# Attention of a hybrid decoder block on pairs of heads, with one step for mask, scale and row extreme, and the merge's rounding on ScalarE

## What is computed

```
merged = sigmoid(gate_a) * (out_a @ w_proj_a) + sigmoid(gate_b) * (out_b @ w_proj_b)
x = x + gate1 * (merged @ w_out)
h2 = rms_norm(x) * (1 + scale2) + shift2
x = x + gate2 * (square(relu(h2 @ w_mlp1 + b_mlp1)) @ w_mlp2 + b_mlp2)
```

## Time and profile before

| | us |
|---|---|
| median of three runs (963.65 to 968.84) | 968.44 |
| the profiled execution, its own time | 967.11 |
| its span, first to last instruction | 965.4 |
| TensorE busy | 878.1 (91%) |
| VectorE busy | 464.7 (48%) |
| ScalarE busy | 335.9 (35%) |
| mean granted TensorE clock, share of full | 0.950 |

### The profile page before, as it was taken

One profiled execution on the slowest core, in us unless ns is written; L12 is line 12 of the kernel. 1 busy time (PEld: TensorE's weight loads), 2 busy tenths in 40 slices (PEclk: granted clock), 3 DMA queues, 4 the chain that ended last, 5 costly groups with the idle time before them and its releaser, 6 DMA issues.

```text
span 965.4 us, 10903 instructions
## 1 busy us (share of the span) xinstructions
PE 878.1 (91%) x3855; PEld 688.1 (71%) x3855; DVE 464.7 (48%) x763; ACT 335.9 (35%) x495; POOL 233.0 (24%) x125
## 2 busy tenths in 40 slices
PE   3799899899877977988899996999999999999998
PEld 2577578687766764655568874688888888888886
DVE  4914789791887784444429764643211122221000
ACT  2634452453123313665512223434312124442211
POOL 3024233334000000000000000264444444444440
PEclk9699999999989977989889998999999999999999
DMA  9912323423111112222226653263233233333302
GB/s 358 254 54 72 82 66 87 107 54 101 25 38 27 44 27 82 66 83 71 66 66 202 199 187 108 68 195 108 89 93 103 87 97 99 89 107 97 99 22 87
DMA packets 144551, 95.69 MB, mean 99 GB/s; under 512 B 8199, under 2 KB 138629, under 8 KB 143493
## 3 DMA queue, kind: packets, MB, share of 16 engines
q1 hardware_dynamic: 143104, 95.18, 33.2%
q10 hardware_dynamic: 1412, 0.07, 0.1%
HBM read 93.13 MB, written 2.10 MB: 99 GB/s over the span
## 4 chain that ended last, share of the span: by engine, by line
PE 75%; DVE 18%; DMA 2%; ACT 2%; issue 2%; SPq 0%; DVEq 0%; ACTq 0%
PE bank L1100 19%; PE bank L1101 19%; PE bank L1102 19%; PE bank L1241 3%; PE bank L1242 3%; PE bank L1243 2%; DMA ada_raw<-in_w_ada 2%; PE bank L1318 2%; PE bank L1344 2%; DVE w_lo L753 2%; DVE hg_at L909 2%; DVE hg_rt L877 1%; DVE rt_k L805 1%; PE bank L1128 1%; DVE ada_acc L972 1%
## 5 line engine op out<-in xcount | busy, mean ns | idle before, releaser
L407 POOL TENSOR_TENSOR w_lo<-w_raw,w_hi 128x1024 fp32r<-128x1024 f32 x90 | 224.1, 2489 | 703.7 <-ACT w_hi L461 703.7
L1100 PE MATMUL bank<-h_hi,w_hi 128*128 128x512 f32 x544 | 219.3, 403 | 14.0 <-DVE h_lo L783 13.5
L1101 PE MATMUL bank<-h_lo,w_hi 128*128 128x512 f32 x544 | 213.6, 393 | 0.0
L1102 PE MATMUL bank<-h_hi,w_lo 128*128 128x512 f32 x544 | 213.3, 392 | 0.0
L461 ACT ACTIVATE w_hi<-w_raw 128x1024 fp32r<-128x1024 f32 x126 | 132.7, 1053 | 166.1 <-PE bank L1102 163.5
L1100 PEld LDWEIGHTS bank<-h_hi,w_hi 128*128 128x128 f32 x544 | 102.9, 189 | 45.7 <-issue 16.9
L1101 PEld LDWEIGHTS bank<-h_lo,w_hi 128*128 128x128 f32 x544 | 103.3, 190 | 21.9 <-issue 1.7
L1102 PEld LDWEIGHTS bank<-h_hi,w_lo 128*128 128x128 f32 x544 | 103.2, 190 | 21.7
L1100 PE MATMUL bank<-u_hi,w_hi 128*128 128x512 f32 x256 | 100.0, 391 | 0.0
L1102 PE MATMUL bank<-u_hi,w_lo 128*128 128x512 f32 x256 | 99.7, 389 | 0.0
L1101 PE MATMUL bank<-u_lo,w_hi 128*128 128x512 f32 x256 | 99.6, 389 | 0.0
(11 more groups left out here) (212 smaller groups left out, 1087.1 us busy)
## 6 DMA issues: line engine op xcount, KB each, us to landing
w_raw<-in_w_mlp SPq DMA_DIRECT2D x128, 256.0 KB, 3.0
w_raw<-in_w_in SPq DMA_DIRECT2D x88, 256.0 KB, 3.3
ada_even<-in_w_ada SPq DMA_DIRECT2D x20, 512.0 KB, 4.7
ada_raw<-in_w_ada SPq DMA_DIRECT2D x8, 1024.0 KB, 9.1
ada_odd<-in_w_ada SPq DMA_DIRECT2D x8, 512.0 KB, 4.5
w_raw<-in_w_out SPq DMA_DIRECT2D x16, 256.0 KB, 3.0
x_nat<-in_x SPq DMA_DIRECT2D x4, 512.0 KB, 6.3
w_raw<-in_w_proj_a SPq DMA_DIRECT2D x8, 256.0 KB, 2.8
```

Of the source, the lines that this page charges most:

```text
L407: nc.gpsimd.tensor_tensor(w_lo[:, s], w_raw[:, s], w_hi[:, s].bitcast(F32), ALU.subtract).then_inc(lo_ready, 1)
L1100: mm(bank[b][:], w_hi[:, slot, j], rhs_hi(i), start=f, stop=False)
L1101: mm(bank[b][:], w_hi[:, slot, j], rhs_lo(i), start=False, stop=False)
L1102: end = mm(bank[b][:], w_lo[:, slot, j], rhs_hi(i), start=False, stop=l)
```

## The change

- Attention goes by pairs of heads. Logits of heads 2p and 2p+1 alternate, widest query block first (512, 512, 384, 384, ... columns), into four banks instead of two; the fifth waits for VectorE to have taken the first.
- VectorE's one step now adds the mask, scales by -1/8 and takes the row minimum, so the step that scaled the maximum (L996) is gone, and ScalarE's exponential waits for its own block alone. Reciprocals are one per block (eight of 128 x 1 for a pair) in place of one of 128 x 4 per head.
- Transposes of a pair alternate between banks 2 and 3, a block of the gate projection between them; values of the two heads alternate within the unit of a pair, on the two column halves of the array. `prT` is doubled.
- TensorE does gate block 8 before the logits of pair 0, block 9 after them, block 8+2p between the transposes of pair p-1, block 9+2p after the logits of pair p, and the b halves of projections 0 and 1 and parts of their a halves between the transposes of the last pair and around its values.
- The eight groups of two in the first projections become one each; GpSimd is not touched. Two slices of `w_ada` are asked for at the start, then 3, 3 and 2 `ada_add` stand before the mask steps of pairs 1, 2 and 3, three after the last pair, and one in each of merges 1 to 5; the buffers move, so that the second is free from the start.
- The merge: the rounding to `h_hi` is taken by ScalarE, and `split_lo` and `ada_add` stand between the sum and `h_lo`.

The core of the diff (new helper functions in full where the text speaks of them):

```diff
+        ADA_PAIR = [0, 0, 3, 6, 8, 11]
+        LOGIT_BANK = [[6, 7, 2, 3], [6, 7, 4, 5]]
+        def heads(p):
+            return [(2 * s + e, TB - 1 - s, e) for s in range(TB) for e in range(2)]
 # SyncE
             load_ada(0)
-            for m in range(KC):
-                if m + 1 < KC:
-                    load_ada(m + 1)
-                load_proj(m)
+            load_ada(1)
+            for p in range(1, PAIRS + 1):
+                load_proj(2 * p - 2)
+                load_proj(2 * p - 1)
+                for i in range(ADA_PAIR[p] + 2, ADA_PAIR[p + 1] + 2):
+                    load_ada(i)          # waits for ada_add(i - 2)
 # ScalarE
+            for p in range(PAIRS + 1):
+                if p:
+                    turned(p - 1)        # eight copies bank -> prT
+                if p < PAIRS:
+                    gate(KC + 2 * p, sig_b[:, 2 * p])
+                    for t, qb, e in heads(p):
+                        act.wait_ge(logit_masked, 8 * p + t + 1)
+                        w = pr[:, e, OFF_Q[qb]:OFF_Q[qb] + (qb + 1) * P]
+                        nc.scalar.activation(w, w, ACT.Exp, scale=-1.0, bias=..., accum_out=...)
+                    gate(KC + 2 * p + 1, sig_b[:, 2 * p + 1])
+                if p:
+                    oa_head(p - 1)
+            for m in range(KC):
+                act.wait_ge(group_done, G[U_P + m + 1])
+                split_hi(U_P + m + WS)
+                act.wait_ge(sum_ready, m + 1)
+                nc.scalar.activation(h_hi[:, m], sig_a[:, m], ACT.Copy).then_inc(mh_ready, 1)
 # VectorE
+            for p in range(PAIRS + 1):
+                if p:
+                    split_lo(U_M + KC + WS + 2 * p - 2)
+                    split_lo(U_M + KC + WS + 2 * p - 1)
+                if p >= 2:
+                    oa_low(p - 2)
+                if p < PAIRS:
+                    for i in range(ADA_PAIR[p], ADA_PAIR[p + 1]):
+                        ada_add(i)
+                    if p:
+                        dve.wait_ge(prob_turned, 8 * p)
+                    for t, qb, e in heads(p):
+                        v.tensor_tensor_reduce(out=pr[...], in0=bank[...], in1=score[:, qb, 0:n],
+                            scale=-(HD ** -0.5), scalar=-TAKEN, op0=ALU.add, op1=ALU.min, accum_out=...)
+                    for t, qb, e in heads(p):
+                        dve.wait_ge(exp_done, 8 * p + t + 1)
+                        step(v.reciprocal(s, s))
+                        v.tensor_scalar(w, w, s, None, ALU.mult).then_inc(prob_ready, 1)
+            mod_add(0)
+            ada_add(KC)
+            oa_low(PAIRS - 1)
+            ada_add(KC + 1)
+            ada_add(KC + 2)
             for m in range(KC):
                 dve.wait_ge(group_done, G[U_P + m + 1])
                 v.tensor_tensor(sa, bank[b][:], sa, ALU.mult)
                 step(v.tensor_tensor(sb, bank[b + 1][:], sb, ALU.mult))
-                step(v.tensor_tensor(sa, sa, sb, ALU.add))
-                step(v.tensor_copy(mh, sa))
+                v.tensor_tensor(sa, sa, sb, ALU.add).then_inc(sum_ready, 1)
+                if m < KC - 1:
+                    split_lo(U_P + WS + m)
+                if 1 <= m <= 5:
+                    ada_add(10 + m)
+                dve.wait_ge(mh_ready, m + 1)
                 v.tensor_tensor(ml, sa, mh.bitcast(F32), ALU.subtract).then_inc(merged_ready, 1)
-                split_lo(U_P + WS + m)
-                ada_add(KC + m)
 # TensorE
+            gate_blocks(KC, 0, 8)
+            pe.wait_ge(ort_ready, BH)
+            logits(0)
+            gate_blocks(KC + 1, 0, 8)
+            for p in range(1, PAIRS):
+                j = KC + 2 * p
+                def filler(t):           # called before the first and after each of the eight t
+                    if t == 0:
+                        gate_blocks(j, 0, 2)
+                    elif 2 <= t <= 7:
+                        gate_blocks(j, t, t + 1)
+                turn_probs(p - 1, filler)
+                logits(p)
+                gate_blocks(j + 1, 0, 8)
+                values(p - 1)
+            ... last pair: turn_probs with proj_blocks(0, 4, 8), (1, 4, 6), (1, 6, 8), (0, 0, 2)
+            mod_columns(0)
+            values(PAIRS - 1)
+            proj_blocks(0, 2, 3)
+            proj_blocks(1, 0, 3, True)
+            pe.wait_ge(oa_ready, PAIRS)
+            proj_blocks(0, 3, 4, False, True).then_inc(group_done, 1)
+            proj_blocks(1, 3, 4, False, True).then_inc(group_done, 1)
+            for m in range(2, KC):
+                pe.wait_ge(merged_ready, m - 1)
+                pe.wait_ge(lo_ready, U_P + m + 1)
+                proj_blocks(m, 4, 8, True, True)
+                proj_blocks(m, 0, 4, True, True).then_inc(group_done, 1)
```

More of the change, by code:

```diff
@@ L627, in _ @@
             gate(2 * BH - 1, sig_a[:, 2 * BH - 1])
[L630 to L653, removed]
-                        act.wait_ge(ob_ready, BH)
-                    gate(KC + h, sig_b[:, h])
@@ L658, in _, with turned @@
[L658 to L663, removed]
+            def turned(p):
+                if p:
+                    act.wait_ge(pv_done, p)
+                for t, kb, e in heads(p):
+                    act.wait_ge(prob_turned, 8 * p + t + 1)
+                    w = T - kb * P
+                    nc.scalar.activation(prT[:, e, OFF_K[kb]:OFF_K[kb] + w], bank[2 + t % 2][:, kb * P:T],
+                                         ACT.Copy).then_inc(probT_ready, 1)
@@ L1005, in _ @@
[L1005 to L1015 removed]
+                            out=pr[:, e, OFF_Q[qb]:OFF_Q[qb] + n], in0=bank[LOGIT_BANK[p > 0][t % 4]][:, 0:n],
@@ new lines, in turn_probs @@
+            def turn_probs(p, filler):
+                filler(0)
+                for t, kb, e in heads(p):
+                    if 8 * p + t >= 2:
+                        pe.wait_ge(probT_ready, 8 * p + t - 1)
+                    pe.wait_ge(prob_ready, 8 * p + t + 1)
+                    for qb in range(kb, TB):
+                        o = OFF_Q[qb] + kb * P
+                        end = nc.tensor.transpose(bank[2 + t % 2][:, qb * P:(qb + 1) * P], pr[:, e, o:o + P],
+                                                  ident[:])
+                    end.then_inc(prob_turned, 1)
+                    filler(t + 1)
@@ new lines, in values @@
+            def values(p):
+                if p:
+                    pe.wait_ge(oa_ready, p)
+                else:
+                    pe.wait_ge(lin_evac, G[U_M + KC + 1])
+                pe.wait_ge(probT_ready, 8 * (p + 1))
+                for kb in range(TB):
+                    w = T - kb * P
+                    for e in range(2):
+                        g = 2 * p + e
+                        end = mm(bank[0][HD * e:HD * (e + 1), kb * P:T], v_nat[:, kb, g * HD:(g + 1) * HD],
+                                 prT[:, e, OFF_K[kb]:OFF_K[kb] + w], start=kb == 0, stop=kb == TB - 1)
+                end.then_inc(pv_done, 1)
@@ new lines, in proj_blocks @@
+            def proj_blocks(m, j0, j1, start=False, stop=False):
+                n = U_P + m
+                b = 4 + 2 * (m % 2) + j0 // AC
+                rhs_hi, rhs_lo = (oa_hi, oa_lo) if j0 < AC else (ob_hi, ob_lo)
+                for j in range(j0, j1):
+                    k, w = j % AC, j == j1 - 1 and stop
+                    mm(bank[b][:], w_hi[:, n % WS, j], rhs_hi[:, k], start=start and j == j0, stop=False)
+                    mm(bank[b][:], w_hi[:, n % WS, j], rhs_lo[:, k], start=False, stop=False)
+                    end = mm(bank[b][:], w_lo[:, n % WS, j], rhs_hi[:, k], start=False, stop=w)
+                return end
```

181 lines of the change are left out of this document (68 added, 113 removed).

## The result

The changed kernel takes 927.19 us (median of 4, 924.24 to 928.68) against 968.25 in the same comparison: a ratio of 0.9575, interval 0.9554 to 0.9596, 41 us off. Two more measurements of the same code gave 927.6 (0.9559 to 0.9615) and 929.95 (0.9597 to 0.9635). The third interval lies just above the first, for the same code, so a difference of 3 us between two comparisons is not to be read. The forecast of 939 was 9 to 12 us too slow. The range ended at 928, and the three medians (927.2, 927.6, 930.0) lie on both sides of that edge.

The account below looks back on a forecast made before the run. TensorE was taken to bound the projections, and a loop of logits, mask, exponentials and next head to bound attention. 39.4 us gained less 10 for clock gave 29: 967.1 - 29 = 938, stated as 939 against the median; range 928 to 955.

Parts of the forecast that it names:

- The walk: From attention's start to w_out: the engines' ordered lists followed at full clock, putting the start of w_out at 499.8.
- the first mask step of pair 1: In attention: VectorE starts it at 393.0, after slice 2 lands at about 391.7.
- the wait before projection 2: In the tail: block 2 must wait for merge 0, ending near 467, so TensorE stands 4 us.
- The wait for slice 10: In the tail: slice 10 lands at 461.5 and is added by 463.0, making VectorE late for merge 0.
- the clock term: Over the changed stretch: four low-clock pieces costing 3.4 us each, less overlap with waits, taken as 10, range 3 to 18.
- Column halves: In a pair's values: the two heads run beside each other on column halves, 2.3 us instead of 4.6.
- rival 1: In the values: column halves don't overlap, 2.3 us more per pair, 8 us less gain, about 947; chance 0.22.
- Logits on row halves: In a pair's logits: paced by four mask steps of VectorE, 3.3 to 3.7 us in all.
- the rounding on ScalarE: In the merges: takes nothing off by itself, hidden by TensorE's block; saves 0.4 where cover is gone, at merge 0.
- The dropped step on the maximum: In attention: 0.17 us per head, on the path only in that exponentials start with the first mask step.
- rival 2: In attention: the chain of VectorE and ScalarE becomes the bound, attention gives 12 us less, 951; chance 0.16.
- my 39.4: At w_out's start: gain at full clock, 539.2 - 499.8 = 39.4 us, before the clock deduction.

Follow-up runs that it names:

- e4: Changed kernel with gate block 8 put back behind the logits of pair 0; 940.0 us.
- v3: Changed kernel with three pairs of banks in the first projections, slices earlier, gate block 9 before the logits of pair 0; 922.8 and 920.0 us.
- e1: Changed kernel with the values of a pair head by head, so neighbours use the same column half; 935.0 us.
- e2: Changed kernel with logits, mask steps, exponentials and transposes of a pair head by head; 930.7 us.
- e3: Changed kernel with the merge's rounding back on VectorE and ScalarE's copy gone; 930.7 us.
- b1: Kernel before with only mask, scale and row minimum in one step, each exponential waiting for its own block; 968.2 us, ratio 1.001.
- v2: Changed kernel with the w_ada slices moved earlier so that VectorE never waits for a buffer; 929.7 us.
- e5: Changed kernel with the gate block whole before the transposes in pairs 1 to 3, not in pieces between them; 930.7 us.
- b2: Kernel before with only gate block 8 moved ahead of the first logits, heads still one by one; 968.1 us, ratio 0.9996.
- v1_three_banks: Changed kernel with three pairs of banks in turn in the first projections, so block 2 need not wait for merge 0; 922.55 us.
- v1_again: Second measurement of the changed kernel with three pairs of banks in the first projections; 924.2 us.
- v4: Changed kernel with slices earlier and gate block 9 before the logits of pair 0, but two pairs of banks; 927.2 us.

## Why the prediction was wrong

- **The walk was right to 2.5 us, in part by luck.** `w_out` was forecast at 499.8, 137.2 us behind the last small sum, at full clock; the three profiles of the changed kernel say 134.7 to 135.4 with their low pieces taken off. Shifted by the 2.1 us of the later start, the first mask step of pair 1 was said to be at 395.1 and came at 396.2, that of pair 2 415.1 and 416.1 (both hold what the low piece at 377.9 cost, up to 1.7 us), the end of merge 0 469.1 and 468.4. TensorE bound the pairs from there on (19.9 from the first mask step of pair 1 to that of pair 2, and again to that of pair 3, forecast 20.0); the wait before projection 2 was 3.4 to 3.7, forecast 4. The end of the first projections' last piece before that wait, 465.0 in both, is luck: TensorE began the sums at 456.5 and not at 455.3, but the walk counted eight blocks of three matmuls behind the values where the code has six, 1.4 us too many. The wait for slice 10 that the walk had there was 0.1 to 0.5 us in the three profiles.
- **The step that failed is the one on the clock**: four pieces of 3.4 us lost each, taken at 10 together. In the three profiles of the changed kernel 3.4, 10.2 and 10.2 us were at 1.2 GHz, in one, two and three pieces, which cost 1.7 to 5.1. They lay at three of the four places that I had picked (none in the sums and values), but I had sized each by the piece at 471 to 478, behind a pause of 3.4 us. Where TensorE now runs thin or waits 1.7 us or less, pieces are 3.4 us long or absent (one was 6.8, behind the wait of 1.70). Behind the wait of 3.4 to 3.7 before projection 2 there was none, or one of 3.4. So the clock term was too large by 5 to 8 us; which of the places bring a low piece in a given execution stays open. With 137.2 + 3.4 in place of 137.2 + 10 the forecast would have been 932, and with the walk's 2 us, 930. The 3 that remain are of the size by which executions differ: the forecast added 1.3 because the profiled execution of before lay under its median, and that of after lay 1.5 over its own. e4, with a pause of 6.6 us, was followed by 6.8 low; v3, whose longest wait is 0.8, had none in two profiles.
- **The range was cut too tight at that end.** Its lower bound, 928, was the walk with no low clock at all and no error in the walk; a walk of thirty steps that is 2 us long puts 926 in reach. On which side of 928 a median of this code falls is chance: two fell under it by less than 1 us, one over it by 2.
- **Column halves** (rival 1, chance 0.22): decided by e1, they overlap, with sixteen passes in 2.38 us where neighbours use different halves and 3.93 where they don't. The Trainium skill (TensorEngine Tiling (Array Packing), Key Properties) says that different tiles load and multiply in parallel; the trace after agrees.
- **Logits on row halves** were rightly given almost nothing (e2), and so was the rounding on ScalarE, as far as e3 can tell. The dropped step on the maximum was forecast to be on the path only a little; alone it is worth nothing (b1).
- **VectorE and ScalarE as the bound** (rival 2, 0.16): in pairs 2 and 3 VectorE waits 1.22 and 5.21 us for the first logits, and TensorE only 0.25 for a mask step, which speaks against it. In pair 1 it holds in a small way: the chain that ended last runs there through slice 2, which landed 5.5 us after it was asked for and not 4.7, and TensorE waits 0.86 for the mask step behind it. v2, in which VectorE waits for no slice, is 1.4 us shorter at full clock.
- **Where 40 us came from**, by the table: 25.5 at full clock (160.2 to 134.7) and 14.7 from the clock (16.4 lost to it in the stretch before, 1.7 after; in the other two profiles of the changed kernel 5.1, which leaves 11.3). The clock was not a cost of the change but a third of its gain, give or take; my 39.4 already held that part, since it set a walk at full clock against the old stretch as it ran, and the 10 gave two thirds of it back. Of the 25.5, some 6.5 is the first gate block in its place (e4), 6 the values side by side (e1), 3 the pieces between transposes (e5); the remaining 10 was not tried alone, and its cause is not shown. It is the size of the three pauses of 3.36 us in the old loop (10.1 of the 17.1 in the earlier trace rows), of which 0.86, 0.25 and 0.25 are left now that two heads share them.

## What to carry to other kernels

Write the in-order lists of the engines side by side with durations from the trace and walk them to the end of the changed stretch: here that came within 2.5 us of 137. Cost the clock apart from it and as a range: behind pauses of about 3.4 us these runs had from 0 to 10.2 us at half clock (0 to 6.8 in the new order), and behind waits of 1.7 us or less in the new order nothing or 3.4, once 6.8. Count a pause that goes as worth its length and about half of the low piece behind it, where one stood. One filler moved into a pause can open another where it stood (b2 won nothing): a gain of this kind belongs to the whole order, so test the parts inside the new order and not only in the old one. And check a walk at several points of the trace, not at its end alone: here two errors of over 1 us hid each other at one of them.

## What the runs showed of the hardware

- The granted clock falls at other places in each execution of one code. The part ahead of the stretch, all but the same in all kernels made from the changed one, took 360.4 to 365.2 us, and these two ends are executions of one code (v1_three_banks and v1_again), with 34.1 and 51.2 us of it at 1.2 GHz. Busy time by stretch of two executions of the changed kernel, clocks 0.93 and 0.95:

```profile
0.00:364.71 364.71, 308.24 (x1410) 240.81 (x1411) 255.61 (x428) 130.80 (x192) 81.19 (x65) 0.93 0.32 93
```

```profile
0.00:360.65 360.65, 301.41 (x1410) 235.70 (x1411) 254.37 (x428) 130.70 (x192) 81.23 (x65) 0.95 0.33 94
```

- A wait of 3.2 to 3.8 us before projection 2 stands in ten profiles of eight kernels (the changed one three times, e1 to e5, v2, v4): a low piece began during it or within 2 us of its end in all but two (the first of the changed kernel, and e5). In the four profiles of v1 and v3, which lack the wait, none did. So the wait brings the low clock most of the time, not always; what decides it was not found.
- Two heads' values with neighbours on different column halves take 2.4 us in 16 passes, as long as one head's 8. With neighbours on the same column half they take 3.9 us, less than twice the 2.3 of one head alone.
